# Second attention of a hybrid encoder layer: gate sums as one 128-row product for each head ahead of the mask, query-key products last

## Chip, cores and metric

One Trainium2 chip, one core. The metric is the device time of one execution of the kernel in microseconds. The program computes two layers of a streaming encoder for 512 frames.

## What is computed

The reference, cut to the part in question. Each of the two layers runs two attentions of 8 heads; the second adds a cumulative forget-gate sum to its scores.

```python
def block_attention(q, k, v, scale, diag_mask, cum=None):
    for q0 in range(0, S, Q_BLOCK):                      # Q_BLOCK = 128, S = 512
        q1 = q0 + Q_BLOCK
        s = einsum('bhqd,bhkd->bhqk', q[:, :, q0:q1], k[:, :, :q1]) * scale
        if cum is not None:
            s = s + cum[:, :, q0:q1, None] - cum[:, :, None, :q1]
        mask = concatenate([ones((Q_BLOCK, q0)), diag_mask], axis=1)
        p = softmax(where(mask, s, -inf), axis=-1)
        outs.append(einsum('bhqk,bhkd->bhqd', p, v[:, :, :q1]))
...
log_f = log_sigmoid(f_logit + b_forget[l])
cum = cumsum(log_f, axis=1).transpose(0, 2, 1)           # 8 heads x 512
o_b = block_attention(qf, kf, vf, fox_scale, frame_mask, cum)   # head size 64
```

The term `cum[q]` is the same for a whole row of the softmax and falls out of it, so the kernel adds only the term of the keys. The rest of a layer is an input projection (1024 to 6312 columns), the first attention, a convolution, gates, an output projection and a feed-forward part, nearly all of it matrix products.

## The kernel before

The activations stand transposed in SBUF, 128 channels to a tile and 512 frames as columns. A large product is made of float parts: each operand is split into a high and a low part (`h_hi`, `h_lo`, `w_hi`, `w_lo`, type fp32r), and three products (high-high, low-high, high-low) of 128x128 weights with 512 columns are summed in a PSUM bank. The order of work on every engine is written out by hand, and semaphores alone tie the engines together.

Both attentions of a layer run in one loop of 64 steps (`for g in range(0, STEPS, 2)` in the tensor block), two steps an iteration. A step is one head and one query block q, so its scores have w = 128(q + 1) columns. Steps 0 to 31 are the first attention, steps 32 to 63 the second, by pairs of heads in the order `FOX_ORDER`: both heads of a pair with q = 0, then with q = 3, 1 and 2. An iteration g issues on TensorE, in this order:

- the scores of steps g + 2 and g + 3 (`logits`); in the second attention one call of `fox_logits` makes both, one for each head of the pair, in two score banks
- four to six units of the projection that feeds the second attention and the gates (`unit`, L1981), three products of 512 columns in each
- the transposes of the softmax weights of steps g and g + 1 (`turn`, L1993)
- after each pair of heads the value products (`values`, L2014), 64 output rows for each of the two heads; they come directly ahead of the scores with q = 1

`fox_logits` makes, for two heads of a pair: two plain float products of queries and keys (L1952), for which the heads lie in partitions 0 to 63 and 64 to 127 of `q_t` and `k_t`; two products that add the gate sums (L1955); and two bf16 products that add the mask to the last 128 columns (L1957). Plain float products appear in a trace as two records each.

The gate sums stand in `cum_x` (128 x 512, fp32r): the low parts of the 8 heads in rows 0 to 7, the high parts in rows 32 to 39, and both again in rows 64 to 71 and 96 to 103 for the second head of a pair; all other rows are zero. `head_of` holds for each pair a 128-column stationary operand with ones in the rows of the head that is meant, in all of its columns. ScalarE writes it in each layer from `head_col` (one column for each pair), as it writes the high parts (step 10) and the second copy of the low parts (step 18); GpSimd subtracts the high from the whole sum (L725). The other engines in the loop: VectorE takes the maximum of each score row (L1356) and normalises (L1328), ScalarE computes the exponentials (L858) and copies transposed weights out (L831), and between these they split the projection's weights and run the convolution's taps.

The semaphores that the change touches: `cum_hi` and `cum_low` count the high and the low parts, `cum_put` ScalarE's two last writes, `exp_done` frees a score bank, `evac_done` tells (at the first group of a pair) that the pair's keys have been copied out, `score_done` releases the maximum.

Of the kernel before, what the change touches and what calls it, by code (L numbers as in the profile page):

```python
# [21 lines left out]
F32 = mybir.dt.float32  # L22
F32R = mybir.dt.float32r
BF16 = mybir.dt.bfloat16
I32 = mybir.dt.int32
ALU = mybir.AluOpType
# [3 lines left out]
P = 128  # L30
# [5 lines left out]
PAIRS = HEADS // 2  # L36
# [80 lines left out]
assert min(STEP_TAPS) >= 0 and sum(FEED_UNITS) == 8 * len(FEED) + 6 and FEED_END[-1] == 61  # L117
P_AT = (0, P, 3 * P, 6 * P)
FOX_ORDER = ((0, 0, 0), (1, 0, P), (0, 3, 2 * P), (1, 3, 6 * P), (0, 1, 10 * P), (1, 1, 0), (0, 2, 2 * P), (1, 2, 5 * P))
CUM_ROWS = 32 + HEADS  # L120
CUM_HI = ROPE
P_T_STEP = 3 * P
P_T_SIZE = 3 * P_T_STEP + T
# [116 lines left out]
def trunk(nc, dram, out):  # L240
# [4 lines left out]
    def at(name, off, shape, dt=F32):  # L245
        return nc.alloc_sbuf_tensor_at(name, shape, dt, offset=off)

    def sb(name, shape, dt=F32):
        size = int(np.prod(shape[1:])) * (2 if dt == BF16 else 4)
        t = at(name, free[0], shape, dt)  # L250
        free[0] += size + (-size) % 32
        assert free[0] <= nc.sbuf_usable_end, (name, free[0] - nc.sbuf_usable_end)
        return t
# [43 lines left out]
    r0 = free[0]  # L297
    free[0] += 91 * KB
    assert free[0] <= nc.sbuf_usable_end, free[0] - nc.sbuf_usable_end
    head_col = sb("head_col", [P, PAIRS])  # L300
    q_t = at("q_t", r0, [P, HEADS, T])
    k_t = at("k_t", r0 + 16 * KB, [P, HEADS, T])
    v_n = at("v_n", r0 + 32 * KB, [P, TT, HEADS * VDIM])
# [18 lines left out]
    misc_t = at("misc_t", r0 + 82 * KB, [P, T])  # L322
    misc_b = at("misc_b", r0 + 88 * KB, [P, T])
    f_sum = at("f_sum", r0 + 66 * KB, [P, T])
    head_of = at("head_of", tmp_off + 6 * KB, [P, PAIRS, P], F32R)
    key_a = at("key_a", r0 + 84 * KB, [P, T])
    key_b = at("key_b", r0 + 86 * KB, [P, T])

# [50 lines left out]
    with ExitStack() as ctx:  # L379
# [5 lines left out]
        def sem(name):  # L385
            return ctx.enter_context(nc.semaphore(name))
# [27 lines left out]
        cum_zero = sem("cum_zero")  # L414
        cum_hi = sem("cum_hi")
        cum_low = sem("cum_low")
        cum_put = sem("cum_put")
        kr_ready = sem("kr_ready")
        misc_half = sem("misc_half")
        misc_ready = sem("misc_ready")  # L420
# [202 lines left out]
        def _(pool):  # L623
# [36 lines left out]
            for l in layers([(sq, SQUARES), (zero, 2), (stat, 6), (pv, HEADS),  # L660
# [40 lines left out]
                if l == 0:  # L701
                    nc.gpsimd.tensor_scalar(cum_x[:], ident[:].unsqueeze(1).broadcast_to([P, TT, P]), 0.0, None, ALU.mult).then_inc(cum_zero, 1)
                    pool.wait_ge(cum_zero, 1)
                    nc.gpsimd.memset(head_col[:], 0.0).then_inc(cum_zero, 1)
                    pool.wait_ge(cum_zero, 2)
                    for n in range(4):
                        first = 32 * n + n // 2
                        nc.gpsimd.tensor_copy(head_col[32 * n:32 * n + HEADS, :],
                                              ident[32 * n:32 * n + HEADS, first:first + HEADS:2]).then_inc(cum_zero, 1)
                        pool.wait_ge(cum_zero, 3 + n)  # L710
                evac.add(CONV_CH + 2)
                for g in range(HEADS):
# [6 lines left out]
                for pair in range(2 * PAIRS):  # L719
                    if pair:  # L720
                        pair_low(pair - 1)
                    if pair == 1:
                        pool.wait_ge(cum_hi, 2 * (l + 1))
                        passed(pool)
                        nc.gpsimd.tensor_tensor(cum_x[32 - CUM_HI:32 - CUM_HI + HEADS, :], f_sum[F, :], cum_x[F, :].bitcast(F32),  # L725
                                                ALU.subtract).then_inc(cum_low, 1)
                        pool.wait_ge(cum_low, l + 1)
# [21 lines left out]
        def _(act):  # L749
# [70 lines left out]
            def attention(l):  # L820
                F = slice(ROPE, MISC)

                def turn(g):
                    act.wait_ge(turn_done, tn.add())
                    if g % 8 == 0:
                        if g:
                            act.wait_ge(pv_done, pv.value)
                        pv.add()
                    _, e, q, _ = step_of(g)
                    to = p_t[e][:, q * P:q * P + (q + 1) * P_T_STEP].rearrange("p (k c) -> p k c", c=P_T_STEP)[:, :, 0:P]  # L830
                    nc.scalar.copy(to, t_bank[g % 2][:, 0:(q + 1) * P].rearrange("p (k q) -> p k q", q=P)).then_inc(turn_out, 1)  # L831

                def pair_out(pair):
                    hi_out = (oa_hi, ob_hi)[pair // PAIRS]
                    act.wait_ge(pv_done, ohi.add())
                    act.wait_ge(o_lo_done, olo.value)
                    olo.add()
                    nc.scalar.copy(o_raw[:], o_bank[:])
                    nc.scalar.copy(hi_out[:, pair % PAIRS, :], o_bank[:]).then_inc(o_hi_done, 1)

                def weights(ended):

                    for n in ended:
                        split(QKV + n + 2)
                        evac.add()

                for g in range(0, STEPS, 2):
                    ended = [n for n, end in enumerate(FEED_END) if g - 4 <= end < g - 2]
                    if g >= 4:
                        turn(g - 4)  # L850
                        turn(g - 3)
                    if g == STEPS - 2:
                        weights(ended)
                    for step in (g, g + 1):
                        act.wait_ge(max_ready, mx.add())
                        _, _, q, p_at = step_of(step)
                        w = (q + 1) * P
                        nc.scalar.activation(p_b[:, p_at:p_at + w], s_bank[score_slot(step)][:, 0:w], ACT.Exp,  # L858
                                             bias=neg_max[:, step % 4:step % 4 + 1],
                                             accum_out=row_sum[:, step % 4:step % 4 + 1]).then_inc(exp_done, 1)  # L860
                    if g < STEPS - 2:
                        weights(ended)
                    if g % 8 == 4 and g > 8:
                        pair_out(g // 8 - 1)
                    if g == 10:
                        act.wait_ge(cum_ready, l + 1)
                        for e in range(2):
                            nc.scalar.copy(cum_x[64 * e + CUM_HI:64 * e + CUM_HI + HEADS, :], f_sum[F, :]).then_inc(cum_hi, 1)
                    if g == 14:
                        nc.scalar.copy(head_of[:], head_col[:].unsqueeze(2).broadcast_to([P, PAIRS, P])).then_inc(cum_put, 1)  # L870
                    if g == 18:
                        act.wait_ge(cum_low, l + 1)
                        nc.scalar.copy(cum_x[96 - CUM_HI:96 - CUM_HI + HEADS, :], cum_x[32 - CUM_HI:32 - CUM_HI + HEADS, :].bitcast(F32)).then_inc(cum_put, 1)
                    if g - 4 in V_TURN_STEPS:
                        act.wait_ge(vt_done, vt.add())
                        v = V_TURN_STEPS[g - 4]
                        nc.scalar.copy(v_n[:, :, v * P:(v + 1) * P],
                                       o_bank[:].rearrange("p (t c) -> p t c", t=TT)).then_inc(v_ready, 1)
                turn(STEPS - 4)
                turn(STEPS - 3)  # L880
                for n, end in enumerate(FEED_END):
                    if STEPS - 4 <= end < STEPS - 2:
                        split(QKV + n + 2)
                        evac.add()
                turn(STEPS - 2)
                turn(STEPS - 1)
                pair_out(2 * PAIRS - 1)
# [962 lines left out]
        def _(pe):  # L1850
# [77 lines left out]
            def attention(l, rhs):  # L1928
# [10 lines left out]
                def fox_logits(g):  # L1939

                    pair, q = g // 8 - PAIRS, step_of(g)[2]
                    if g % 8 == 0:
                        pe.wait_ge(evac_done, fed + FEED.index(f"k{pair}") + 1)
                    if g == STEPS // 2:
                        pe.wait_ge(cum_put, 2 * (l + 1))
                    ex.add()
                    pe.wait_ge(exp_done, ex.add())
                    w = (q + 1) * P
                    b = [s_bank[score_slot(g + e)] for e in range(2)]
                    for e in range(2):  # L1950
                        rows = slice(NOPE * e, NOPE * (e + 1))
                        nc.tensor.matmul(b[e][:, 0:w], q_t[rows, 2 * pair, q * P:w], k_t[rows, 2 * pair, 0:w], start=True, stop=True)  # L1952
                    for e in range(2):
                        rows = slice(64 * e, 64 * e + CUM_ROWS)
                        nc.tensor.matmul(b[e][:, 0:w], head_of[rows, pair, :], cum_x[rows, 0:w], start=False, stop=True, skip_group_check=True)  # L1955
                    for e in range(2):
                        nc.tensor.matmul(b[e][:, q * P:w], ident_b[:], mask_b[:], start=False, stop=True,  # L1957
                                         skip_group_check=True).then_inc(score_done, 1)

                def logits(g):  # L1960
# [371 lines left out]
```

## Time and profile before

| | |
|---|---|
| median of 3 runs | 1699.58 us (1699.39 to 1701.07) |
| the profiled execution, as timed | 1700.26 us |
| its span in the profile | 1698.4 us |
| TensorE products busy | 1683.3 us, 99% |
| TensorE weight loads | 1401.0 us, 82% |
| VectorE | 1202.7 us, 71% |
| ScalarE | 768.0 us, 45% |
| GpSimd | 194.7 us, 11% |

The span is the time between the first and the last instruction of the core; the time as measured is a little longer. PE is TensorE's products, PEld its weight loads (they overlap the products), DVE is VectorE, ACT ScalarE, POOL GpSimd. The end of a matrix product in a trace is modelled and neighbours overlap, so starts are compared, not ends.

### The profile page before, as it was taken

The page shows a single profiled execution, that of the slowest core. Times are in us where ns is not written, and L with a number is a line of the kernel's source. Part 1 is how long each engine was busy: PE and PEld are TensorE (multiplying, and loading weights), DVE is VectorE, ACT ScalarE, POOL GpSimd, SP SyncE. Part 2 cuts the span into 40 slices and gives each one's busy share as a digit, 9 for nine tenths or more (in the row PEclk, how much of TensorE's full clock was granted, in tenths as well). Part 3 has the DMA queues.
Part 4 walks back from the last instruction along what each step waited for, and adds up shares of the span by engine and source line. Part 5 has one row for each costly group of instructions (what it writes and reads, how often), then busy time and mean ns, then how long its engine had stood idle before and what let it go on. Part 6 is the DMA issues. An engine that isn't in the chain of part 4 may idle for free.

```text
span 1698.4 us, 24436 instructions
## 1 busy us (share of the span) xinstructions
PE 1683.3 (99%) x9060; PEld 1401.0 (82%) x9060; DVE 1202.7 (71%) x1699; ACT 768.0 (45%) x1236; POOL 194.7 (11%) x125
## 2 busy tenths in 40 slices
PE   9999999999999999999999999999999999999998
PEld 7777777878788899988878777778788889999887
DVE  6898887966547887763259998877755488888422
ACT  4655454344342555552245555452533334446222
POOL 0830000010020000000126210000101100000010
PEclk9999999999999999999999999999999999999999
DMA  6341211333433233333333321213333333334332
GB/s 168 81 109 50 62 52 37 101 94 94 117 91 99 84 104 111 112 96 94 96 92 71 94 62 50 57 44 106 93 99 112 98 88 100 100 99 119 90 91 74
DMA packets 277166, 152.53 MB, mean 90 GB/s; under 512 B 30356, under 2 KB 276366, under 8 KB 277068
## 3 DMA queue, kind: packets, MB, share of 16 engines
q1 hardware_dynamic: 276760, 150.96, 31.8%
q8 instruction: 63, 1.03, 0.2%
q10 hardware_dynamic: 308, 0.25, 0.1%
q14 instruction: 35, 0.29, 0.1%
HBM read 149.09 MB, written 2.10 MB: 89 GB/s over the span
## 4 chain that ended last, share of the span: by engine, by line
PE 92%; DVE 4%; ACT 1%; DMA 1%; issue 1%; POOL 1%; SPq 0%; ACTq 0%; DVEq 0%; POOLq 0%
PE bank L1867 52%; PE bank L2182 16%; PE bank L1981 12%; PE bank L2014 2%; PE bank L1993 2%; PE bank L1936 2%; PE bank L1952 1%; PE bank L2267 1%; DMA raw<-in_w_ffn_up 1%; DVE w_lo L1238 1%; PE bank L1921 1%; POOL ln_acc L640 1%; DMA raw<-in_w_in 1%; PE bank L1908 1%; PE bank L1899 0%
## 5 line engine op out<-in xcount | busy, mean ns | idle before, releaser
L764 ACT CAST w_hi<-raw 128x1024 fp32r<-128x1024 f32 (+3 forms) x243 | 223.7, 921 | 464.7 <-PE bank L1867 458.0
L1238 DVE TENSOR_TENSOR w_lo<-raw,w_hi 128x1024 fp32r<-128x1024 f32 (+3 forms) x243 | 264.7, 1089 | 155.7 <-ACT w_hi L764 154.6
L1867 PE MATMUL bank<-h_hi,w_hi 128*128 128x512 f32 x672 | 267.2, 398 | 0.7 <-DVE w_lo L1238 0.4
L1867 PE MATMUL bank<-h_hi,w_lo 128*128 128x512 f32 x672 | 262.1, 390 | 0.0
L1867 PE MATMUL bank<-h_lo,w_hi 128*128 128x512 f32 x672 | 262.0, 390 | 0.0
L1315 DVE SCALAR_TENSOR_TENSOR c_acc<-u_pad,dwk_l,c_acc 128x512 f32<-128x512 f32 x240 | 189.4, 807 | 0.4
L1867 PEld LDWEIGHTS bank<-h_hi,w_hi 128*128 128x128 f32 x672 | 126.2, 188 | 35.2 <-issue 6.5
L2182 PE MATMUL bank<-t_hi,w_hi 128*128 128x256 f32 x512 | 145.2, 284 | 3.5 <-DVE tmp L1766 3.3
L1867 PEld LDWEIGHTS bank<-h_lo,w_hi 128*128 128x128 f32 x672 | 126.3, 188 | 26.8 <-issue 1.9
L1867 PEld LDWEIGHTS bank<-h_hi,w_lo 128*128 128x128 f32 x672 | 126.2, 188 | 26.6
L2182 PE MATMUL bank<-t_hi,w_lo 128*128 128x256 f32 x512 | 144.7, 283 | 0.0
L2182 PE MATMUL bank<-t_lo,w_hi 128*128 128x256 f32 x512 | 144.6, 282 | 0.0
L1981 PE MATMUL bank<-h_hi,w_hi 128*128 128x512 f32 x304 | 130.9, 431 | 0.0
L1867 PE MATMUL bank<-f_hi,w_hi 128*128 128x512 f32 x330 | 129.3, 392 | 0.0
L1867 PE MATMUL bank<-f_hi,w_lo 128*128 128x512 f32 x330 | 128.6, 390 | 0.0
L1867 PE MATMUL bank<-f_lo,w_hi 128*128 128x512 f32 x330 | 128.6, 390 | 0.0
L1981 PE MATMUL bank<-h_hi,w_lo 128*128 128x512 f32 x304 | 119.1, 392 | 0.0
L1981 PE MATMUL bank<-h_lo,w_hi 128*128 128x512 f32 x304 | 118.7, 390 | 0.0
L1648 DVE TENSOR_TENSOR w_lo<-raw,w_hi 128x1024 fp32r<-128x1024 f32 x66 | 80.8, 1224 | 43.3 <-ACT w_hi L1073 43.3
L1276 DVE TENSOR_TENSOR tmp<-bank,rstd_x 128x512 f32<-128x512 f32 x76 | 52.2, 689 | 83.3 <-PE bank L1867 75.8
L2182 PE MATMUL bank<-h_hi,w_hi 128*128 128x256 f32 x384 | 108.9, 284 | 0.0
L2182 PE MATMUL bank<-h_hi,w_lo 128*128 128x256 f32 x384 | 108.8, 283 | 0.0
(312 smaller groups left out, 3526.6 us busy)
## 6 DMA issues: line engine op xcount, KB each, us to landing
raw<-in_w_in SPq DMA_DIRECT2D x96, 512.0 KB, 3.8
raw<-in_w_ffn_gate SPq DMA_DIRECT2D x44, 512.0 KB, 3.8
raw<-in_w_ffn_up SPq DMA_DIRECT2D x44, 512.0 KB, 4.3
raw<-in_w_ffn_down SPq DMA_DIRECT2D x32, 512.0 KB, 3.6
raw<-in_w_out SPq DMA_DIRECT2D x16, 512.0 KB, 3.6
raw<-in_w_ffn_down SPq DMA_DIRECT2D x16, 384.0 KB, 3.2
raw<-in_w_bo_a SPq DMA_DIRECT2D x16, 256.0 KB, 2.8
raw<-in_w_bo_b SPq DMA_DIRECT2D x16, 256.0 KB, 2.7
```

Source lines behind the costliest of these rows:

```text
L640: nc.gpsimd.tensor_tensor(acc[:], acc[:], ring[i % 2][:], ALU.add).then_inc(sq_added, 1)
L764: last = nc.scalar.copy(to, of)
L1238: last = nc.vector.tensor_tensor(to, of, part.bitcast(F32), ALU.subtract)
L1276: return nc.vector.tensor_tensor(to, s_bank[b][rows, :], by[rows, :], ALU.mult)
L1315: ins = nc.vector.scalar_tensor_tensor(c_acc[:, c, :], u_pad[:, c, k:k + T], dwk_l[:, c, k:k + 1], c_acc[:, c, :], ALU.mult, ALU.add)
L1648: nc.vector.tensor_tensor(as_k(w_lo[slot]), of, as_k(w_hi[slot]).bitcast(F32), ALU.subtract).then_inc(lo_done, 1)
L1867: ins = nc.tensor.matmul(bank_t[0:rows, :], wt[slot][:, w], x, start=first and k == 0 and p == 0, stop=last and k == k_tiles - 1 and p == 2)
L1936: nc.tensor.matmul(s_bank[score_slot(g)][:, 0:w], q_t[0:rows, head, q * P:w], k_t[0:rows, head, 0:w], start=True, stop=True).then_inc(scor ...
L1981: ins = nc.tensor.matmul(bank_t[:], wt[(QKV + n) % SPLIT][:, w], x, start=k == 0 and p == 0, stop=k == DT - 1 and p == 2, skip_group_check ...
L1993: ins = nc.tensor.transpose(t_bank[g % 2][:, k * P:(k + 1) * P], p_b[:, at_k:at_k + P], ident[:])
L2014: ins = nc.tensor.matmul(o_bank[e * VDIM:(e + 1) * VDIM, k * P:T], v_n[:, k, head * VDIM:(head + 1) * VDIM], p_t[e][:, k * (P_T_STEP + P): ...
L2182: ins = nc.tensor.matmul(bank_t[:, m * (T // 2):(m + 1) * (T // 2)], wt[:, w], x, start=first and m == 0 and k == 0 and p == 0, stop=last ...
```

## The change

In `fox_logits` the order becomes gate sums, mask, query-key products. The gate product of a head now uses all 128 rows of `cum_x`, one product after the other, and `head_col`, which now has one column for each of the 8 heads, is read as the stationary operand with a step of zero in its columns. Thus `head_of` and the second copies of the sums are no longer made. The wait for a pair's keys stands behind the masks, and `score_done` is told by the query-key products.

```diff
-CUM_ROWS = 32 + HEADS
...
-    head_col = sb("head_col", [P, PAIRS])
+    head_col = sb("head_col", [P, HEADS], F32R)
...
-    head_of = at("head_of", tmp_off + 6 * KB, [P, PAIRS, P], F32R)
...
-                    nc.gpsimd.memset(head_col[:], 0.0).then_inc(cum_zero, 1)
+                    nc.gpsimd.tensor_scalar(head_col[:], ident[:, 0:HEADS], 0.0, None, ALU.mult).then_inc(cum_zero, 1)
                     pool.wait_ge(cum_zero, 2)
-                    for n in range(4):
-                        first = 32 * n + n // 2
-                        nc.gpsimd.tensor_copy(head_col[32 * n:32 * n + HEADS, :],
-                                              ident[32 * n:32 * n + HEADS, first:first + HEADS:2]).then_inc(cum_zero, 1)
+                    for n in range(2):
+                        rows = slice(32 * n, 32 * n + HEADS)
+                        nc.gpsimd.tensor_copy(head_col[rows, :], ident[rows, rows]).then_inc(cum_zero, 1)
                         pool.wait_ge(cum_zero, 3 + n)
...
-                        pool.wait_ge(cum_hi, 2 * (l + 1))
+                        pool.wait_ge(cum_hi, l + 1)
...
                     if g == 10:
                         act.wait_ge(cum_ready, l + 1)
-                        for e in range(2):
-                            nc.scalar.copy(cum_x[64 * e + CUM_HI:64 * e + CUM_HI + HEADS, :], f_sum[F, :]).then_inc(cum_hi, 1)
-                    if g == 14:
-                        nc.scalar.copy(head_of[:], head_col[:].unsqueeze(2).broadcast_to([P, PAIRS, P])).then_inc(cum_put, 1)
-                    if g == 18:
-                        act.wait_ge(cum_low, l + 1)
-                        nc.scalar.copy(cum_x[96 - CUM_HI:96 - CUM_HI + HEADS, :], cum_x[32 - CUM_HI:32 - CUM_HI + HEADS, :].bitcast(F32)).then_inc(cum_put, 1)
+                        nc.scalar.copy(cum_x[CUM_HI:CUM_HI + HEADS, :], f_sum[F, :]).then_inc(cum_hi, 1)
...
                     pair, q = g // 8 - PAIRS, step_of(g)[2]
-                    if g % 8 == 0:
-                        pe.wait_ge(evac_done, fed + FEED.index(f"k{pair}") + 1)
                     if g == STEPS // 2:
-                        pe.wait_ge(cum_put, 2 * (l + 1))
+                        pe.wait_ge(cum_low, l + 1)
                     ex.add()
                     pe.wait_ge(exp_done, ex.add())
                     w = (q + 1) * P
                     b = [s_bank[score_slot(g + e)] for e in range(2)]
                     for e in range(2):
-                        rows = slice(NOPE * e, NOPE * (e + 1))
-                        nc.tensor.matmul(b[e][:, 0:w], q_t[rows, 2 * pair, q * P:w], k_t[rows, 2 * pair, 0:w], start=True, stop=True)
-                    for e in range(2):
-                        rows = slice(64 * e, 64 * e + CUM_ROWS)
-                        nc.tensor.matmul(b[e][:, 0:w], head_of[rows, pair, :], cum_x[rows, 0:w], start=False, stop=True, skip_group_check=True)
+                        head = head_col[:, 2 * pair + e:2 * pair + e + 1].broadcast_to([P, P])
+                        nc.tensor.matmul(b[e][:, 0:w], head, cum_x[:, 0:w], start=True, stop=True)
                     for e in range(2):
                         nc.tensor.matmul(b[e][:, q * P:w], ident_b[:], mask_b[:], start=False, stop=True,
+                                         skip_group_check=True)
+                    if g % 8 == 0:
+                        pe.wait_ge(evac_done, fed + FEED.index(f"k{pair}") + 1)
+                    for e in range(2):
+                        rows = slice(NOPE * e, NOPE * (e + 1))
+                        nc.tensor.matmul(b[e][:, 0:w], q_t[rows, 2 * pair, q * P:w], k_t[rows, 2 * pair, 0:w], start=False, stop=True,
                                          skip_group_check=True).then_inc(score_done, 1)
```

## Rows read from the trace of the kernel before

**Rows 1.** The page, busy us of each engine, share of the span.

```profile
PE 1683.3 (99%) x9060; PEld 1401.0 (82%) x9060; DVE 1202.7 (71%) x1699; ACT 768.0 (45%) x1236; POOL 194.7 (11%) x125
```

**Rows 2.** Windows view: length, busy of PE, PEld, DVE, ACT, POOL (instructions), PEclk, DMA.

```profile
196.00:297.00 101.00, 101.00 (x569) 73.55 (x568) 81.12 (x163) 48.45 (x124) 7.32 (x5) 1.00 0.18 48
```

**Rows 3.** Waits of PE, whole span: us in total, times, longest.

```profile
PE bank L1936 <- ACT p_b L858: 0.9, 2, 0.5
```

**Rows 4.** Who waited for the normalised weights (L1328): us, times.

```profile
  PEld bank L1993: 0.5, 2
```

**Rows 5.** Timeline of PE, score groups of 128, 512, 256, 384 columns: start, us.

```profile
197.33 0.49 PE L1993 MATMUL bank<-ident,p_b 128*128 128x128 f32 x3
197.75 0.49 PE L1952 MATMUL bank<-k_t,q_t 64*128 64x128 f32 x4
198.00 0.31 PE L1955 MATMUL bank<-cum_x,head_of 40*128 40x128 f32 x2
198.24 0.29 PE L1957 MATMUL bank<-mask_b,ident_b 128*128 128x128 bf16 x2
...
198.65 0.40 PE L1981 MATMUL bank<-h_lo,w_hi 128*128 128x512 f32 x1
...
202.72 1.13 PE L1952 MATMUL bank<-k_t,q_t 64*128 64x512 f32 x4
203.28 0.81 PE L1955 MATMUL bank<-cum_x,head_of 40*128 40x512 f32 x2
...
204.43 0.39 PE L1981 MATMUL bank<-h_lo,w_hi 128*128 128x512 f32 x1
...
209.72 0.60 PE L2014 MATMUL bank<-p_t,v_n 128*64 128x256 f32 x6
210.26 0.70 PE L1952 MATMUL bank<-k_t,q_t 64*128 64x256 f32 x4
...
211.42 0.40 PE L1981 MATMUL bank<-h_lo,w_hi 128*128 128x512 f32 x1
...
214.89 0.92 PE L1952 MATMUL bank<-k_t,q_t 64*128 64x384 f32 x4
...
216.32 0.39 PE L1981 MATMUL bank<-h_lo,w_hi 128*128 128x512 f32 x1
```

**Rows 6.** Timeline of PE's weight loads in the 384-column group: start, us, idle before.

```profile
214.89 0.30 PEld L1952 LDWEIGHTS bank<-k_t,q_t 64*128 64x128 f32 x4 [0.17 <-issue]
...
215.91 0.11 PEld L1957 LDWEIGHTS bank<-mask_b,ident_b 128*128 128x128 bf16 x2 [0.39 <-issue]
```

**Rows 7.** Timeline of PE behind the last value products of the first layer.

```profile
293.63 0.60 PE L2014 MATMUL bank<-p_t,v_n 128*64 128x256 f32 x6
294.17 0.50 PE L1867 MATMUL bank<-h_hi,w_hi 128*128 128x512 f32 x1
294.50 0.40 PE L1867 MATMUL bank<-h_lo,w_hi 128*128 128x512 f32 x1
294.74 0.39 PE L1867 MATMUL bank<-h_hi,w_lo 128*128 128x512 f32 x1
```

**Rows 8.** Timeline of PE, transposes ahead of a score product of the first attention.

```profile
124.81 0.38 PE L1993 MATMUL bank<-ident,p_b 128*128 128x128 f32 x2
125.03 1.67 PE L1936 MATMUL bank<-k_t,q_t 100*128 100x384 f32 x4
```

**Rows 9.** Timeline of PE, two products of 256 columns in the feed-forward part.

```profile
600.03 0.28 PE L2182 MATMUL bank<-t_hi,w_hi 128*128 128x256 f32 x1
600.15 0.28 PE L2182 MATMUL bank<-t_lo,w_hi 128*128 128x256 f32 x1
```

**Rows 10.** The tile cum_x and the tile head_of: duration ns min/median/max, first and last start.

```profile
L868 ACT CAST cum_x<-f_sum x4: 617/618/622, 140.0 to 976.5; 8x512 fp32r<-8x512 f32 x4
L873 ACT CAST cum_x<-cum_x x2: 619/620/620, 162.0 to 997.9; 8x512 fp32r<-8x512 f32 x2
...
L870 ACT CAST head_of<-head_col x2: 606/606/607, 153.3 to 989.2; 128x512 fp32r<-128x512 f32 x2
```

More of the change, by code:

```diff
@@ L416, in trunk @@
         cum_low = sem("cum_low")
-        cum_put = sem("cum_put")
         kr_ready = sem("kr_ready")
```

## The prediction

> **What bounds the kernel now.** I read the busy shares first [rows 1]: TensorE is busy for 99% of the span. The windows view of the first layer's second-attention stretch says the same of the place that is edited [rows 2]: TensorE 101.00 of 101.00 us, at full granted clock, beside 81.12 us of VectorE and 48.45 us of ScalarE. The list of who waited for whom names almost nothing: over the whole span TensorE's score products waited 0.9 us for an exponential [rows 3], and the transposes of the weights 0.5 us for the normalised weights [rows 4]. So TensorE sets the end, and what the change costs or saves is what it costs or saves in TensorE's order of instructions. For that the timeline is the view, read from start to start: a busy figure is no help here, since the shown durations of neighbouring products overlap.
>
> One score group is read so [rows 5], in the 128-column one. The last of three transposes starts at 197.55 (197.33 plus two steps of 0.11, the rest of 0.49 being its own 0.27). 0.20 us later the query-key products start: four records, two passes for each head, and one x4 row, since the two heads sit in rows 0 to 63 and 64 to 127 and start together. The two gate products (40 rows each, the same two halves) also share a row, and follow in step; then two masks; the second product of the next projection starts at 198.65. From last transpose to there: 1.10 us (0.20 + 0.90). The same reading gives 1.36 us for 256 columns, 1.63 for 384 and 1.91 for 512 (gap of 0.20 plus 1.16, 1.43, 1.71). There are 32 groups, eight of each width, equal to within 0.01 us. From 128 to 512 columns that is 0.27 us for each 128 columns: twice 0.107 for the two query-key passes and 0.053 for the gate sums, which thus cost one stream for two heads. The 0.107 also shows in the start of the gate row behind that of the first pass: 0.25 us at 128 columns, 0.56 at 512.
>
> **Prices needed.** I call k the width in units of 128 columns; values below 10 ns come from these rates.
> - A full-array product of this split float type: starts 0.23 us apart at 512 columns (294.50 to 294.74) [rows 7] and 0.12 at 256 [rows 9]; so 0.053k + 0.013, but no closer than a weight load, 0.11, the step of the transposes [rows 5].
> - A change of how the array is divided. From transposes (128 rows) to a score product of 100 rows, which keeps the full array, takes 0.11 (124.81 + 0.11 = 124.92 to 125.03) [rows 8]; transposes to 64 rows takes 0.20 [rows 5]; the value products (64 columns) to a full-array product take 0.20 too [rows 7]. A float pass of 128 columns streams for 0.107 of that, so a change drains 0.096.
> - After such a change the weight load is not hidden: the first full product behind the values is followed by the next after 0.336 us in place of 0.23 [rows 7], 0.107 more. In the loads' own timeline the query-key load starts with its product at 214.89, having waited 0.17, and that of the mask at 215.91, 0.39 after the last one ended [rows 6]: nothing is loaded across a change. The mask's small load (shown 0.11 for two, against 0.30 for the four of the query-key products) hardly shows.
> - Without a change, a full float product behind a short one starts its successor 0.34 after that short one (mask at 198.31, second projection product at 198.65) [rows 5]: 0.115 plus its own step.
>
> Beside this the Trainium skill (TensorEngine Tiling, Key Properties) says that changing the tiling mode, not just the tile, drains TensorE; the trace agrees with its 0.20 against 0.11 us. That rule speaks against the change only where it adds a mode change, which is behind the values, below.
>
> **The change, part by part.** *Order inside a group.* Now the order is change to halves, query-key, gates in halves, change to full, masks, projection. Afterwards: gates (full), masks (full), change to halves, query-key, change to full, projection. The number of changes stays two where a transpose comes before. The gates are no longer side by side, and the second change is now followed by a projection product with its whole load exposed, where it was a mask with a small one. In ns, for k = 1, 3, 4:
> - last transpose to second gate: 224 (two loads), 288, 342
> - second gate to first mask: 67, 173, 227
> - between masks: 66
> - second mask to query-key: 53 + about 100 = 153. No row has a mask ahead of a change; it could be the 203 of the transposes if that gap were a fixed one (+1.6 us over 32 groups); I take 153, since the value products with another stream agree with the sum of stream and drain
> - first query-key pass with its load, 7 for the second head: 220, 434, 541
> - second pass and drain: 203, 417, 524
> - first projection product, load exposed: 336
>
> Sums 1269, 1867 and 2189, against 1098, 1631 and 1909 now: +171, +236, +280.
>
> *Behind the values.* All eight 256-column groups follow value products [rows 5]. There the gates add a third change: 202 to the first gate, 229 to the second (107 exposed load + 122), 120 to the mask, then 66, 153, 328, 310, 336. Sum 1744 against 1362: +382.
>
> Eight of each: 8 x (171 + 382 + 236 + 280) = 8 x 1069 ns = **+8.6 us**, all on the path.
>
> *Stationary operand.* The gates' weights are now one column read 128 times with a step of zero, in place of a stored copy. No TensorE row shows such a read. The nearest is ScalarE's making of that copy, which reads in this way: 606 ns for 512 elements, beside 618 for 512 plain ones [rows 10]. So zero extra. From below nothing can be gained, the load keeps its 128 columns; from above, a load of double length would expose, for k = 1 to 4, about 0.21, 0.30, 0.16 and 0.11 us: 8 x 0.78 = 6.2 us.
>
> *Removed ScalarE work.* In each layer the expanded copy, one of two copies of the sums and the copy of the low part go: 0.6 us each, 3.7 us in all [rows 10]. ScalarE is half idle [rows 2]; only the 0.9 us for which TensorE waited on it could come back [rows 3], and those waits are in the first attention. Zero. The GpSimd set-up of the head columns loses two small copies; nothing of TensorE waits there. Zero.
>
> *Waits.* The wait for the last copy of the sums becomes one for the subtraction before it, earlier, so it can't be worse; the wait for the pair's keys moves behind the masks and is over now already, so it gives nothing. The scores are told as ready at the end of the query-key products: at 512 columns about 1.76 us after the last transpose (342 + 227 + 66 + 153 + 541 + 427), against about 1.62 now. VectorE's maximum, ScalarE's exponential and the normalising stand behind that, and then the transposes; but a whole further iteration, with four to six units of three projection products (0.68 us a unit), lies in between. Their wait of 0.5 us over both layers shows that it is enough [rows 4]. Cost zero; uncovered it would be 0.14 x 32 = 4.5 us.
>
> The sum against the profiled execution (span 1698.4 us, 1700.26 as timed): 1708.9; the median of the runs is 0.7 lower, so 1708.1.
>
> **Rivals.**
> 1. *The loads are hidden after all.* The new order puts masks ahead of the halves, and the loads of the query-key products, of the first projection product and of the gates behind the values overlap what runs. Then 32 x (0.107 + 0.107) + 8 x 0.107 = 7.7 us come back: 1700.5, no measurable difference. Against it: in [rows 6] and [rows 7] no load crossed a change. For it: only that no row has just this order. Beside it stands the Trainium skill (TensorE: Matmul & The Clock Gate, Part 2, Step-by-step), by which loads are pulled ahead where row groups don't conflict or a background buffer is the target; the trace shows that inside a mode and not across one.
> 2. *Faster: the changes cost nothing in the new order.* Place: into and out of the query-key pair. Rival 1's 7.7 us and the drains, 0.096 x (64 + 8) = 6.9 us, would be saved: 14.6 - 8.6 = 6.0 us faster, 1693.6. It decides against my sign once more than 8.6 of the 14.6 us are saved. Every one of the 32 gaps ahead of a group, and both behind the last values, is 0.20 us, so little speaks for it.
> 3. *The zero-step load is slow.* Doubled, as above: 1714.3.
> 4. *A new wait for the scores*, 4.5 us on top: 1712.6.
>
> **How the numbers follow.** My forecast 0.83; rival 1 0.06; rival 2 0.02; rival 3 0.05; rival 4 0.04. Of the forecast's own terms the open ones are 1.6 us (the gap behind the mask) upwards and, downwards, some 30 ns a group where a first load or a mask's 13 ns is better hidden, 1 us, with partial hiding of the projection's load (up to 3.4 us). So the range runs from 1704.7 to 1712.0; it leaves out rivals 1 to 3. The measurement tells 0.2%, 3.4 us, from no change: slower 0.91, same 0.06, faster 0.03.
>
> **What would show it.** In the timeline after: two gate products with starts apart by their width, no longer one pair; 0.15 from second mask to query-key; a first projection product that starts 0.20 to 0.52 behind the last pass, with 0.34 to the next; behind the values 0.20 and then 0.23. From last transpose to second projection product 1.27, 1.87, 2.19, and from last value product 1.74. If the gates start 0.2 apart at 128 columns, rival 3 holds; if the projection's load starts during the query-key pass, rival 1; a wait of the transposes above some us, rival 4.

## The result, and the profile after

The change makes the kernel slower by half a per cent. Its median is 1709.07 us (1707.57 to 1709.69, 5 runs) beside 1701.05 us before (1699.39 to 1705.22, 5 runs); the ratio is 1.0051, 95% interval 1.0041 to 1.0062, that is 7.0 to 10.5 us. The forecast was +8.6 us and 1708.1; its base was 1699.58, the median of the first three runs before.

The page after: busy us of each engine. TensorE still fills 99% of the span; its products are busy for 8.7 us more, in the same number of them.

```profile
span 1707.8 us, 24422 instructions
...
PE 1692.0 (99%) x9060; PEld 1405.1 (82%) x9060; DVE 1202.3 (70%) x1699; ACT 766.3 (45%) x1230; POOL 195.0 (11%) x123
```

The timeline of TensorE in four score groups after, for 128, 512, 256 and 384 columns (start, us), the counterpart of [rows 5]. In each the gates (L1940) and the masks (L1942) come first, then the query-key products (L1948), then the projection (L1972); L1984 are the transposes, L2005 the value products.

```profile
197.57 0.27 PE L1984 MATMUL bank<-ident,p_b 128*128 128x128 f32 x1
197.59 0.42 PE L1940 MATMUL bank<-cum_x,head_col 128*128 128x128 f32 x2
197.85 0.28 PE L1942 MATMUL bank<-mask_b,ident_b 128*128 128x128 bf16 x2
198.07 0.49 PE L1948 MATMUL bank<-k_t,q_t 64*128 64x128 f32 x4
198.49 0.50 PE L1972 MATMUL bank<-h_hi,w_hi 128*128 128x512 f32 x1
198.83 0.39 PE L1972 MATMUL bank<-h_lo,w_hi 128*128 128x512 f32 x1
...
202.69 0.27 PE L1984 MATMUL bank<-ident,p_b 128*128 128x128 f32 x1
202.72 0.71 PE L1940 MATMUL bank<-cum_x,head_col 128*128 128x512 f32 x2
203.26 0.28 PE L1942 MATMUL bank<-mask_b,ident_b 128*128 128x128 bf16 x2
203.48 1.13 PE L1948 MATMUL bank<-k_t,q_t 64*128 64x512 f32 x4
...
204.88 0.40 PE L1972 MATMUL bank<-h_lo,w_hi 128*128 128x512 f32 x1
...
210.48 0.28 PE L2005 MATMUL bank<-p_t,v_n 128*64 128x128 f32 x2
210.69 0.50 PE L1940 MATMUL bank<-cum_x,head_col 128*128 128x256 f32 x2
...
212.21 0.40 PE L1972 MATMUL bank<-h_lo,w_hi 128*128 128x512 f32 x1
...
215.27 0.49 PE L1984 MATMUL bank<-ident,p_b 128*128 128x128 f32 x3
215.51 0.60 PE L1940 MATMUL bank<-cum_x,head_col 128*128 128x384 f32 x2
...
217.35 0.39 PE L1972 MATMUL bank<-h_lo,w_hi 128*128 128x512 f32 x1
```

From the last transpose, or the last value product, to the second projection product that is 1.26 us (197.57 to 198.83), 2.19, 1.73 and 1.86, where it was 1.10, 1.91, 1.36 and 1.63. Summed over all 32 groups from the timeline's starts, the stretch takes 56.31 us after and 48.01 us before: +8.30 us. This sum is the measure used below; it repeats to a few hundredths of a microsecond (three executions with the change's order in the groups: 56.31, 56.32 and 56.33), where the span of the same kernel moved by 1.4 us (1707.8 and 1706.4).

The weight loads of the 384-column group after, the counterpart of [rows 6] (start, us, idle before):

```profile
215.95 0.12 PEld L1942 LDWEIGHTS bank<-mask_b,ident_b 128*128 128x128 bf16 x2 [0.16 <-issue]
216.17 0.30 PEld L1948 LDWEIGHTS bank<-k_t,q_t 64*128 64x128 f32 x4
217.01 0.19 PEld L1972 LDWEIGHTS bank<-h_hi,w_hi 128*128 128x128 f32 x1 [0.55 <-issue]
```

The projection's first load begins at 217.01, at the very time at which its product is shown to begin, after 0.55 us in which the load side did nothing. Before, the small load of the masks stood in that place.

### The profile page after: what moved, and what is told of

The parts are those of the page before. It is cut to its first block, busy times and chain, and to the rows that moved or that the text cites. A ratio compares the mean times of both kernels' runs of the same rounds, so it can differ in the third digit from the quotient of the medians.

```text
span 1707.8 us, 24422 instructions
## 1 busy us (share of the span) xinstructions
PE 1692.0 (99%) x9060; PEld 1405.1 (82%) x9060; DVE 1202.3 (70%) x1699; ACT 766.3 (45%) x1230; POOL 195.0 (11%) x123
## 4 chain that ended last, share of the span: by engine, by line
PE 91%; DVE 4%; DMA 2%; ACT 1%; issue 1%; POOL 1%; SPq 0%; ACTq 0%; DVEq 0%; POOLq 0%
PE bank L1857 51%; PE bank L2173 16%; PE bank L1972 12%; PE bank L2005 2%; PE bank L1984 2%; PE bank L1926 2%; PE bank L1948 1%; DMA raw<-in_w_ffn_up 1%; PE bank L2258 1%; DVE w_lo L1228 1%; PE bank L1911 1%; PE bank L1940 1%; POOL ln_acc L637 1%; DMA raw<-in_w_in 1%; PE bank L1898 1%
## 5 line engine op out<-in xcount | busy, mean ns | idle before, releaser
L1972 PE MATMUL bank<-h_hi,w_hi 128*128 128x512 f32 x304 | 131.7, 433 | 0.0
L1972 PE MATMUL bank<-h_hi,w_lo 128*128 128x512 f32 x304 | 119.0, 391 | 0.0
L1972 PE MATMUL bank<-h_lo,w_hi 128*128 128x512 f32 x304 | 118.7, 390 | 0.0
L2173 PE MATMUL bank<-h_lo,w_hi 128*128 128x256 f32 x384 | 108.6, 283 | 0.0
```

The source lines that it names most:

```text
L1972: ins = nc.tensor.matmul(bank_t[:], wt[(QKV + n) % SPLIT][:, w], x, start=k == 0 and p == 0, stop=k == DT - 1 and p == 2, skip_group_check ...
L2173: ins = nc.tensor.matmul(bank_t[:, m * (T // 2):(m + 1) * (T // 2)], wt[:, w], x, start=first and m == 0 and k == 0 and p == 0, stop=last ...
```

## The experiments

Each kernel was run in alternation with the kernel before, except where a single execution is named. The group sum is that of the 32 score groups, from the last product ahead of a group to the second projection product behind it. The array is divided in one of three ways here: whole (128 rows), in halves (two heads in 64 rows each), or, for the value products, in 64 columns. A change of division is a step from one of these to another. The diffs of the first three experiments are written in short and show the order of the products only; `score_done` is told by whatever comes last, and in the first the wait for the pair's keys goes ahead of the query-key products again.

**Full-array gates in the old order.** Against the change, only the order is put back.

```diff
-    gates (start=True); masks; query-key (start=False)
+    query-key (start=True); gates (start=False); masks
```

> Full-array gate products as in the change, but the order of before: query-key, gates, mask. My theory (a full-array gate pair can't share its stream and leaves a weight load exposed, wherever it stands): the group from the last transpose to the second projection product takes 1.32, 1.59, 1.92 and 2.24 us for 128, 256, 384 and 512 columns, against 1.10, 1.36, 1.63 and 1.91 before; 8 x (0.22 + 0.23 + 0.29 + 0.33) = +8.5 us against before, the same as the change, though no third change of division is left behind the values. Rival (the new order is what costs, above all the query-key products at the end): with the old order back at most +2 us stay.

1708.26 us (1708.16 to 1709.04), ratio 1.0051 (1.0038 to 1.0064). Group sum 56.45 us, +8.44. The 256-column group behind the value products (L2004), timeline of TensorE:

```profile
210.73 0.27 PE L2004 MATMUL bank<-p_t,v_n 128*64 128x128 f32 x1
210.93 0.70 PE L1942 MATMUL bank<-k_t,q_t 64*128 64x256 f32 x4
211.57 0.50 PE L1945 MATMUL bank<-cum_x,head_col 128*128 128x256 f32 x2
211.91 0.28 PE L1947 MATMUL bank<-mask_b,ident_b 128*128 128x128 bf16 x2
...
212.32 0.39 PE L1971 MATMUL bank<-h_lo,w_hi 128*128 128x512 f32 x1
```

1.59 us from 210.73 to 212.32, against 1.73 in the new order: the third change of division is gone here. The other widths pay 0.05 us each instead, since the gates' own load is now exposed behind the change (in the 128-column group 1.32 us, against 1.26). So the old order gives nothing back, and the rival by which the order alone costs is wrong: the gates cost about 8 us in the full-array form, in either place.

**Full-array gates first, masks last.** Against the change, the masks alone are moved behind the query-key products.

```diff
-    gates; masks; query-key
+    gates; query-key; masks
```

> Full-array gates first as in the change, then query-key, and the masks last as before, so that a mask and not a projection product follows the change back to the full array. My theory (the load exposed there is a term of its own, about 0.1 us a group, and one mask gap of 0.15 goes with the masks): 1.20, 1.48, 1.81 and 2.13 us for a group, +4.9 us against before, 3.5 less than the change. Rival (loads are hidden anyway and only the full width of the gates and the third change behind the values cost): no less than the change, +8.3 us.

1707.66 us (1705.53 to 1708.1), ratio 1.0043 (1.003 to 1.0056); the interval reaches from 5.1 to 9.5 us and does not tell this kernel from the change. The group sum does: 54.65 us, +6.64, so 1.66 us less than the change. The expectation of +4.9 was wrong, and in one width alone: measured were 1.21, 1.68, 1.81 and 2.13 us, so the 1.48 for 256 columns was 0.20 us too small. That is the size of one gap at a change of division, of which these groups have three. The seven steps of this order, 0.20 + 0.22 + 0.21 + 0.33 + 0.31 + 0.07 + 0.34, make 1.68 us, and 8 x (0.10 + 0.32 + 0.18 + 0.22) is 6.6 us. The 128-column group, products and then loads:

```profile
197.53 0.49 PE L1984 MATMUL bank<-ident,p_b 128*128 128x128 f32 x3
197.78 0.42 PE L1940 MATMUL bank<-cum_x,head_col 128*128 128x128 f32 x2
198.13 0.49 PE L1945 MATMUL bank<-k_t,q_t 64*128 64x128 f32 x4
198.55 0.29 PE L1948 MATMUL bank<-mask_b,ident_b 128*128 128x128 bf16 x2
...
198.96 0.39 PE L1972 MATMUL bank<-h_lo,w_hi 128*128 128x512 f32 x1
```

```profile
198.55 0.11 PEld L1948 LDWEIGHTS bank<-mask_b,ident_b 128*128 128x128 bf16 x2
198.62 0.19 PEld L1972 LDWEIGHTS bank<-h_hi,w_hi 128*128 128x128 f32 x1
```

With the masks in between, the projection's load begins with the second mask (198.62) and about half of it is hidden: from the second mask to the second projection product it is 0.34 us, in place of the mask step and the exposed load, 0.07 + 0.34. What follows: the place of the masks is worth 0.05 us a group, 1.7 us in all. It is a term of its own, and a small one.

**Gates in halves, new order.** The kernel before, in which the same products are issued in the order of the change.

```diff
-    query-key; gates in 40 rows side by side; masks
+    gates in 40 rows side by side; masks; query-key
```

> The gates stay in 40 rows side by side as before, but the order is that of the change: gates, mask, query-key. My theory: the gates in halves ahead of full-array masks add two changes of division and another exposed load; a group takes 1.44, 1.70, 1.97 and 2.24 us, 8 x (0.34 + 0.34 + 0.34 + 0.33) = +10.8 us against before, more than the change itself, so that the full-array form is the cheaper one in this order. Rival (only the loss of the shared stream costs): side by side again, the order is free and the time is that of before within 2 us.

1710.8 us, the median of five executions (1710.36 to 1711.52), ratio 1.0065 (1.0052 to 1.0078). A sixth took 7889.87 us, which nothing on record explains; the ratio leaves it out. Group sum 58.97 us, +10.96, with 1.44, 1.70, 1.98 and 2.25 us. The 128-column group:

```profile
197.63 0.49 PE L1994 MATMUL bank<-ident,p_b 128*128 128x128 f32 x3
198.06 0.33 PE L1952 MATMUL bank<-cum_x,head_of 40*128 40x128 f32 x2
198.32 0.28 PE L1954 MATMUL bank<-mask_b,ident_b 128*128 128x128 bf16 x2
198.53 0.49 PE L1958 MATMUL bank<-k_t,q_t 64*128 64x128 f32 x4
...
199.29 0.39 PE L1982 MATMUL bank<-h_lo,w_hi 128*128 128x512 f32 x1
```

The two gates do share a stream again (one row, 0.01 apart), and still it is the slowest: 0.20 us ahead of the gates (197.85, the last transpose, to 198.06), 0.26 to the masks, 0.21 to the query-key products. The order matters as soon as it splits what runs in halves: there are four changes of division in a group now, where there were two. Once the masks stand ahead of the query-key products, the full-array gates are the cheaper ones, by 58.97 - 56.31 = 2.7 us.

**A stored stationary operand for two of the four pairs.** A single execution.

```diff
+                    if g == 14:
+                        nc.scalar.copy(head_of[:], head_col[:, 0:PAIRS].bitcast(F32).unsqueeze(2).broadcast_to([P, PAIRS, P])).then_inc(cum_put, 1)
...
+                        if pair < 2:
+                            head = head_of[:, 2 * pair + e, :]
```

> The change, but for the heads of the first two pairs the gates' stationary operand is a stored copy of 128 columns, written by ScalarE, and for the other two pairs it is the column read with a step of zero; within one execution the two can be set side by side. My theory (the zero step costs nothing): loads of 0.185 to 0.192 us as shown in both, and groups of equal width equal to 0.01 us in all four pairs. Rival (the zero step reads slower): the groups of the first two pairs are shorter, by 0.1 us or more at 128 columns.

1708.5 us; group sum 56.33, +8.32. The gate line by operand (duration ns min/median/max):

```profile
L1947 PEld LDWEIGHTS bank<-cum_x,head_of x32: 186/190/192, 197.5 to 1079.0; 128*128 128x128 f32 x32
...
L1947 PEld LDWEIGHTS bank<-cum_x,head_col x32: 185/190/192, 243.8 to 1124.9; 128*128 128x128 f32 x32
```

The loads have the same length, and the groups of 128 columns take 1.26 to 1.27 us in all four pairs. Reading one column 128 times costs nothing that shows. The expanded copy that it replaces, put back here, costs nothing in the group sum either.

**Masks in halves.** If a change of division is the price, a group that stays in halves throughout should be the cheapest; that was the idea. It does not lower the number of changes, though: the kernel before has two (into the halves, and out of them ahead of the masks), and so has a group all in halves (out of them ahead of the projection). The causal pattern is the same for queries and keys 0 to 63 as for 64 to 127, and for the keys 64 to 127 the row of the mask that its last query doesn't need masks all of the first 64 queries; so each head's mask fits into two products with its own 64 rows and 64 columns each. First with the masks last, as in the kernel before:

```diff
+                nc.vector.memset(ident_b[:, 64:P], 0.0).then_inc(const_ok, 1)
+                nc.vector.memset(ident_s[:, P - 1:P], 0.0).then_inc(const_ok, 1)
+                for h in (0, 64):
+                    rows = slice(h, h + 64)
+                    nc.vector.tensor_copy(ident_b[rows, 0:64], const_sb[rows, h:h + 64]).then_inc(const_ok, 1)
+                    nc.vector.tensor_copy(ident_s[rows, 0:64], const_sb[rows, h + 63:h + 64].broadcast_to([64, 64])).then_inc(const_ok, 1)
+                    nc.vector.tensor_copy(ident_s[rows, 64:P - 1], const_sb[rows, h:h + 63]).then_inc(const_ok, 1)
+                    nc.vector.tensor_copy(mask_b[rows, :], const_sb[rows, 2 * P + h:2 * P + h + 64]).then_inc(const_ok, 1)
+                    nc.vector.scalar_tensor_tensor(mask_s[rows, :], const_sb[rows, h + 63:h + 64].broadcast_to([64, 64]), MASKED,
+                                                   const_sb[rows, 2 * P + h:2 * P + h + 64], ALU.mult, ALU.add).then_inc(const_ok, 1)
...
-                        nc.tensor.matmul(b[e][:, q * P:w], ident_b[:], mask_b[:], start=False, stop=True,
-                                         skip_group_check=True).then_inc(score_done, 1)
+                    for part, (ident_p, mask_p) in enumerate(((ident_b, mask_b), (ident_s, mask_s))):
+                        for e in range(2):
+                            rows = slice(NOPE * e, NOPE * (e + 1))
+                            ins = nc.tensor.matmul(b[e][:, q * P + 64 * part:q * P + 64 * part + 64], ident_p[rows, :], mask_p[rows, :],
+                                                   start=False, stop=True, skip_group_check=True)
```

> The kernel before, but each head's mask is added in the head's own 64 rows: columns 0 to 63 of the last block by one product of 64 rows, columns 64 to 127 by a second one whose 64th row masks the upper 64 queries as a whole. Order as before: query-key, gates, masks; all three now in halves, so that one change of division stands ahead of the group and one behind it. My theory: the two mask steps take 0.03 us each side by side, the change with the projection's load behind it 0.34 in place of it behind full masks; from the end of the gates' stream 0.49 us in place of 0.51: about -0.9 us in all, below what timing tells but to be seen in the summed groups (48.01 us before). Rival (64-column products have a floor near 0.06 us a step): no gain or a loss of up to 1 us.

1698.91 us (1698.65 to 1701.43) against 1699.72, ratio 0.9996 (0.9987 to 1.0005): no difference. Group sum 48.01, the same as before to the hundredth. Its 128-column group:

```profile
198.04 0.31 PE L1965 MATMUL bank<-cum_x,head_of 40*128 40x128 f32 x2
198.18 0.21 PE L1969 MATMUL bank<-mask_b,ident_b 64*128 64x64 bf16 x2
198.22 0.20 PE L1969 MATMUL bank<-mask_s,ident_s 64*128 64x64 bf16 x2
198.69 0.39 PE L1995 MATMUL bank<-h_lo,w_hi 128*128 128x512 f32 x1
```

The saving of 0.9 us did not come. From gates to masks it is 0.14 us where [rows 5] have 0.24 (198.00 to 198.24), since no change stands there. But the change behind the masks has the projection's whole load behind it: 0.46 us from the last mask product to the second projection product, where it was 0.34. The step between the masks gives back the rest, 0.02 us, and the gain and the loss cancel. The step from the first masks to the second takes 0.04 us instead of the 0.03 that I had. It is the rival's outcome (no gain), though at 0.04 and not 0.06 us a step.

Then with these masks ahead of the query-key products, everything else as before:

> The same masks in halves, placed ahead of the query-key products, so that the small bf16 load and not the 0.107 us one stands behind the first change, and the query-key load is partly hidden behind the masks. My theory: query-key products 0.04 us later than now behind the change, 0.07 us saved between gates and projection: about -1.0 us in all (summed groups 47 us against 48.01). Rival (the query-key load starts only when the masks have ended): 0.05 us a group less gain, +0.6 us.

1697.97 us (1697.51 to 1698.5) against 1699.72 for the kernel before, ratio 0.999 (0.9981 to 0.9999). Group sum 47.12, -0.89 us. Its 128-column group and the loads of its 512-column group:

```profile
197.16 0.49 PE L2005 MATMUL bank<-ident,p_b 128*128 128x128 f32 x3
197.59 0.20 PE L1963 MATMUL bank<-mask_b,ident_b 64*128 64x64 bf16 x2
197.63 0.19 PE L1963 MATMUL bank<-mask_s,ident_s 64*128 64x64 bf16 x2
197.66 0.47 PE L1967 MATMUL bank<-k_t,q_t 64*128 64x128 f32 x4
197.88 0.31 PE L1970 MATMUL bank<-cum_x,head_of 40*128 40x128 f32 x2
198.11 0.50 PE L1993 MATMUL bank<-h_hi,w_hi 128*128 128x512 f32 x1
198.45 0.39 PE L1993 MATMUL bank<-h_lo,w_hi 128*128 128x512 f32 x1
```

```profile
202.51 0.10 PEld L1963 LDWEIGHTS bank<-mask_b,ident_b 64*128 64x128 bf16 x2 [0.16 <-issue]
202.53 0.10 PEld L1963 LDWEIGHTS bank<-mask_s,ident_s 64*128 64x128 bf16 x2
202.56 0.30 PEld L1967 LDWEIGHTS bank<-k_t,q_t 64*128 64x128 f32 x4
```

1.07 us from 197.38 to 198.45, against 1.10. The query-key load starts at 202.56, 0.05 us behind the first mask load: within one division it is taken early, while the masks run, where across a change none was. This is the fastest of the kernels here, by 0.1%, which the interval just tells from none. Half of the 1.75 us between the medians is the groups'. In the profiles TensorE waits for VectorE's `tmp` in the feed-forward part for 2.1 us, where it was 3.3 in the kernel before; that wait differs from one execution to the next (see below), so 0.89 us is what these masks are shown to give.

**The change once more.** A single execution.

> The change once more. My theory: the 32 groups sum to 56.31 us again (48.01 before, +8.30), and the 1.1 us by which the span grew beyond them is not of the change: it varies by about 1 us from one execution to the next. Rival (the change costs about 1 us outside the groups): the span is 1707.8 again to 0.2 us.

1708.29 us with a span of 1706.4; group sum 56.32, +8.31. So the groups repeat and the span does not: the 1.1 us by which the first profile of the change had grown beyond its groups (9.4 against 8.3) are from one execution to the next, not from the change. The traces show where. Most of it, 1.06 us, lies between the last group of the first layer and the first of the second, in the feed-forward part, where TensorE waits for VectorE's `tmp` (the first row is the kernel before, the second the change):

```profile
PE bank L2182 <- DVE tmp L1766: 3.3, 3, 1.2
```

```profile
PE bank L2173 <- DVE tmp L1756: 4.0, 4, 1.6
```

In the second execution of the change the same wait is 2.4 us in all.

## Why the prediction was right

The sum was made of terms of one group, and the trace after gives each of them (starts in ns, from the first group of each width; predicted, then measured; "first passes, second head" goes from the first head's first pass to the second head's second):

| term | 128 columns | 256, behind values | 384 | 512 |
|---|---|---|---|---|
| last product to second gate | 224, 170 | 431, 424 | 288, 288 | 342, 346 |
| second gate to mask | 67, 117 | 120, 122 | 173, 181 | 227, 232 |
| between masks | 66, 66 | 66, 66 | 66, 66 | 66, 66 |
| mask to query-key | 153, 149 | 153, 149 | 153, 149 | 153, 149 |
| first passes, second head | 220, 220 | 328, 327 | 434, 434 | 541, 540 |
| last pass to projection | 203, 202 | 310, 305 | 417, 412 | 524, 519 |
| first projection product | 336, 337 | 336, 335 | 336, 335 | 336, 337 |
| whole | 1269, 1261 | 1744, 1728 | 1867, 1865 | 2189, 2189 |

- *TensorE sets the end.* Right. 8.3 us more in its order of instructions became 8 us (medians) to 9.4 us (spans, with the feed-forward wait above). Its waits did not grow where the change is: TensorE waited 0.9 us for an exponential after as before [rows 3].
- *The side-by-side stream of the gates is lost and a load exposed.* Right, and shown in both orders: the full-array form costs 8.3 us in the new order and 8.4 in the old.
- *Split of the 128-column group.* The two gates start earlier and the mask later than I had it (170 and 117 in place of 224 and 67): the first gate is shown 28 ns behind the transpose, though its load begins only then, and the load's time appears ahead of the products behind it. Thus two terms were wrong by 50 ns in opposite directions; their sum was 291, measured 287.
- *The gap behind the mask,* the open term: 149, as taken, and not the 203 of a fixed gap. A change thus costs what still streams and 0.10 us more: 53 + 96 ns here, 107 + 96 behind transposes [rows 5]. By the Trainium skill (TensorEngine Tiling (Array Packing), Key Properties) a change of tiling mode drains TensorE; the traces agree, with these 0.10 us.
- *The third change behind the values.* Right: 203 to the first gate and 221 to the second; 0.37 us a group where the others lose 0.16 to 0.28.
- *The zero-step operand, the removed copies, the moved waits: nothing.* Right for the first by the stored copy. Of the other two nothing is seen in any sum.
- *The range.* Its lower end has a source, the 3.4 us of a partly hidden load. Of its upper end, 1712.0, only 1.6 us have one (the gap behind the mask); the other 2.3 us come from no term. It also leaves out rival 4, at 1712.6, which the prediction doesn't say. Neither mattered here.
- *The rivals.* Loads hidden across a change: no, 0.55 us idle ahead of the projection's load and none started earlier: in all nine traces the first load behind a change of division begins at most 5 ns ahead of its product, while inside a division the median is 223 ns. That also settles the faster rival: every gap at a change keeps its 0.10 us beyond the running stream. The Trainium skill (TensorE: Matmul & The Clock Gate, Part 2, Step-by-step) has loads pulled ahead where row groups don't conflict or a background buffer is the target; the traces show it inside a division (query-key load 0.05 us behind the first mask load, masks in halves first) and in no case across one. A slow zero-step load: no. A new wait for the scores: VectorE's maximum (L1346) did stand idle for them longer, 32.2 us where it was 24.2, but the transposes (L1984) waited for the normalised weights (L1318) no more than before. What the maximum waited for, before and after, and then who waited for the normalised weights after (us and times):

```profile
  PE bank L1957: 24.2, 18
```

```profile
  PE bank L1948: 32.2, 22
```

```profile
  PEld bank L1984: 0.5, 2
```

The last one equals [rows 4]. That it is the slack of a whole iteration between scores and transposes that absorbs the delay is the likely reason, which no run here tests.

What was argued and not tried: that the removed ScalarE and GpSimd work by itself gives nothing in the kernel before; only the reverse, a copy put back into the change, was run.

## What to carry to other kernels

Where TensorE is the bound, count for every reordering how often the division of the array changes and what stands directly behind each change: here a change cost 0.10 us beyond the running stream, and the load of the product behind it was exposed, 0.107 us for a float operand of 128 columns and nearly nothing for bf16 (two masks follow each other in 66 ns, of which 53 are their stream). Splitting a run of halves was the dearest here (+10.96 us). Keeping the whole group in halves gave nothing by itself (48.01 us both ways), since two changes a group stay; with the small-loading product directly behind the first change it gave 0.89 us. And a full-array product is not free for having unused rows, since it gives up the stream that two heads shared. Compare start-to-start sums of the edited stretch: they told 0.9 us and 1.7 us from nothing, where the times of the runs did so hardly or not at all.

## What the runs showed of the hardware that was not expected

- A product's start in the trace can be shown 0.03 us behind the one before it although the load of its weights begins only with that one before (197.57 and 197.59, load from 197.57); the time then appears ahead of the next products. Only sums over several starts are to be trusted.
- Two 64-row mask products in a row, each with its own weights and 64 columns, took 0.04 us a step side by side, in place of the 0.03 that their streams alone suggest.
- A weight load is taken ahead while the division stays and never across a change, in any of the eight kernels: at each of the 96 changes in the trace before (104 after) the load is shown at most 5 ns ahead of its product, while inside a division it is 223 ns in the median and up to 430.
